# A 96-byte buffer that nothing uses, in front of the shared part of SBUF

## The reference, cut to what matters

```python
h = rms_norm(x, mix_norm[l])
kv = mem_n @ w_mem_kv[l]
mixed, mq = attn_mixer(...) if kind == 0 else lru_mixer(...)
mo = memory_attention(mq, mk, mv)
x = x + jnp.concatenate([mixed, mo], axis=-1) @ w_out[l]
x = x + squared_relu_mlp(rms_norm(x, mlp_norm[l]), w_up[l], w_down[l])   # square(relu(h @ w_up)) @ w_down
```

## Time and profile before

| | |
|---|---|
| time before, median of 3 runs | 3184.8 us (3184.78 to 3188.98) |
| the profiled execution's own time | 3187.99 us |
| its span from first to last instruction | 3186.2 us |
| mean granted TensorE clock | 0.991 |
| PE busy | 3074.7 us (97%) |
| DVE, ACT, POOL busy | 53%, 35%, 3% |
| DMA, share of 16 engines | 17.9% |

### The profile page before, as it was taken

The page is one execution under the profiler, slowest core; times in us unless marked ns, Lnnn a source line. Parts: engine busy times, 40 slices in busy tenths (PEclk is TensorE's granted clock), DMA queues, the critical chain, the costliest instruction groups (busy, mean ns, idle before and its releaser), DMA issues.

```text
span 3186.2 us, 34235 instructions
## 1 busy us (share of the span) xinstructions
PE 3074.7 (97%) x14272; PEld 2383.3 (75%) x14272; DVE 1696.9 (53%) x2180; ACT 1105.2 (35%) x1723; POOL 89.9 (3%) x70
## 2 busy tenths in 40 slices
PE   8998999999999999999999999999999999999898
PEld 7884567788888888777777888888887786666566
DVE  7737854544444433589853633333333733666575
ACT  4215632311111111387732311111111525776552
POOL 0004410000000000000000000000000000000000
PEclk9999999999999999999999999999999999999999
DMA  4420011121222211211131111111111131000213
GB/s 150 114 93 1 1 73 34 53 80 66 67 78 73 73 47 40 93 47 47 53 126 33 47 47 47 47 47 50 49 47 47 53 125 32 22 20 20 93 34 125
DMA packets 54507, 190.94 MB, mean 60 GB/s; under 512 B 6288, under 2 KB 6672, under 8 KB 54224
## 3 DMA queue, kind: packets, MB, share of 16 engines
q1 hardware_dynamic: 54352, 188.74, 17.9%
HBM read 172.73 MB, written 14.68 MB: 59 GB/s over the span
## 4 chain that ended last, share of the span: by engine, by line
PE 75%; DVE 12%; ACT 10%; issue 2%; DMA 0%; POOL 0%; SPq 0%; DVEq 0%; ACTq 0%; POOLq 0%
PE PS L262 62%; PE PS L317 3%; DVE sm L854 1%; PE PS L833 1%; DVE p L1459 1%; ACT p L872 1%; PE PS L819 1%; PE PS L2120 1%; PE PS L2137 1%; DVE wsp L224 1%; PE PS L845 1%; ACT wsp L216 1%; PE PS L1028 1%; PE PS L1036 1%; PE PS L2111 1%
## 5 line engine op out<-in xcount | busy, mean ns | idle before, releaser
L262 PE MATMUL PS<-H,wsp 128*128 128x512 f32 x6864 | 1609.6, 394 | 31.6 <-DVE H L421 9.3
L262 PEld LDWEIGHTS PS<-H,wsp 128*128 128x128 f32 x6864 | 1287.3, 189 | 339.0 <-issue 41.3
L262 PE MATMUL PS<-p,wsp 128*128 128x512 f32 (+1 forms) x3840 | 896.7, 393 | 21.6 <-DVE p L1270 15.1
L262 PEld LDWEIGHTS PS<-p,wsp 128*128 128x128 f32 x3840 | 710.8, 189 | 199.1 <-ACT wsp L216 21.5
L216 ACT ACTIVATE wsp<-raw 128x1024 fp32r<-128x1024 f32 (+1 forms) x267 | 277.0, 1041 | 705.4 <-PE PS L262 640.2
L224 DVE TENSOR_TENSOR wsp<-raw,wsp 128x1024 fp32r<-128x1024 f32 (+1 forms) x267 | 321.7, 1207 | 161.1 <-ACT wsp L216 160.7
L1298 DVE TENSOR_TENSOR p<-p,PS 128x1024 f32<-128x1024 f32 x120 | 146.5, 1221 | 393.7 <-PE PS L262 393.7
L1240 ACT ACTIVATE p<-p 128x1024 fp32r<-128x1024 f32 x64 | 67.9, 1062 | 596.7 <-DVE p L1267 596.7
L1264 DVE TENSOR_TENSOR p<-PS,p 128x1024 f32<-128x1024 f32 x64 | 78.4, 1225 | 317.3 <-PE PS L262 317.2
L872 ACT ACTIVATE p<-PS,sm 128x256 f32<-128x256 f32 (+2 forms) x256 | 128.0, 509 | 173.3 <-DVE sm L860 92.8
L1270 DVE TENSOR_TENSOR p<-p 128x1024 fp32r<-128x1024 f32 x64 | 78.5, 1226 | 72.2 <-ACT p L1240 72.2
(11 more groups left out here) (210 smaller groups left out, 2204.7 us busy)
## 6 DMA issues: line engine op xcount, KB each, us to landing
raw<-in_in_dram SPq DMA_DIRECT2D x72, 512.0 KB, 3.5
raw<-in_dn_dram SPq DMA_DIRECT2D x65, 512.0 KB, 3.5
raw<-in_up_dram SPq DMA_DIRECT2D x64, 512.0 KB, 3.5
raw<-in_out_dram SPq DMA_DIRECT2D x42, 512.0 KB, 3.5
p<-in_ada_dram SPq DMA_DIRECT2D x24, 512.0 KB, 4.4
p<-in_x_dram SPq DMA_DIRECT2D x16, 512.0 KB, 7.6
raw<-in_kv_dram SPq DMA_DIRECT2D x16, 512.0 KB, 3.5
spill_dram<-p SPq DMA_DIRECT2D x16, 512.0 KB, 3.0
```

The source lines that it names most:

```text
L262: ins = e.matmul(ps[:, c:c + m], weights(b, j, wi), x[:, c:c + m], start=first and i == 0, stop=end and i == 2)
```

## The change

One line allocates a tile of 24 float32 (96 bytes) per partition after `sm`. No instruction reads or writes it. What is allocated after it, which is the whole shared part, starts 96 bytes further on, at byte 124544, which is 128 bytes past a multiple of 512. No instruction is added, removed or reordered.

```diff
@@ -165,6 +165,7 @@
         sm = sb("sm", [128, 160])
         ident, ones, invf = cf[:, 128:256], cf[:, 256:384], cf[:, 384:385]
         identb, maskL, maskR, maskD, zerob = (cb[:, i * 128:(i + 1) * 128] for i in range(5))
+        sb("line", [128, 24])
         PS = ctx.enter_context(nc.psum_tensor("PS", [128, 8, 512], F32))
         names = [0]
 
```

## The result

The changed kernel takes 3161.53 us, the median of four runs (3159.09 to 3165.07), against 3185.83 us before in the same comparison (3184.78 to 3188.98): a ratio of 0.9921, 95% interval 0.9905 to 0.9937. That is 24.3 us less (20 to 30 by the interval); 3161 and a sum of 23.5 us were forecast. One execution of the kernel before, 5073.69 us at a granted clock of 0.555, is left out of all medians here. The profiled execution took 3159.09 us with a span of 3157.3, where the one before took 3187.99 with 3186.2, so these two lie 28.9 us apart.

The account below looks back on a forecast made before the run. The prediction took PE, busy 97% of the span, to bound the kernel. Its terms, 19.6 + 2.9 + 0.8 + 0.6 - 0.4 = 23.5 us, brought the median from 3184.8 to 3161 us, range 3153 to 3174.

Parts of the forecast that it names:

- MLP down, 15 groups: Down projections of both layers' MLPs: 174 matmuls per group each save 7.5 ns, 1.31 us per group, 19.6 us.
- memory part of both out projections: Out projections, 192 matmuls each with a shared-part tile moving: 7.5 ns saved per matmul, 2.9 us together.
- halves: The 16th down group, done in halves: 111 matmuls on the chain in one piece save 7.5 ns each, 0.8 us.
- memory values: Line 317 with the memory tile stationary: 96 matmuls fall from 233.3 to 226.7 ns, 0.6 us gained.
- memory keys: Products of 256 columns with the shared part moving: 192 matmuls rise 2.1 ns each, 0.4 us lost.
- LRU, `triR`, scores, transposes, DVE, POOL, DMA: LRU and stick-breaking products, plain float32 products, other engines and loads: each counted 0, with small possible gains or losses.
- The anchoring of the wait: MLP groups: PE's wait for DVE's line 1270 grows from 0.81 to about 0.95 us, absorbing what 18 early matmuls save.
- The float32 products: Scores, values and transposes in plain float32 with shared-part tiles: no surcharge to remove, 0; loss end 2 to 2.5 us.
- the 0.9 us of the upper end: First `x` tile's load at the start: at most 0.9 us gained once, counted 0 in the sum.
- Rival 2: F32R streams with the shared part: period longer than 512 bytes, only half fall into step; 3173 us, chance 0.04.
- Rival 1: Shared part: something other than phase, such as its place above byte 124448, sets the 7.5 ns; 3184.8 us, chance 0.09.
- Rival 3: PE's F32R streams with the shared part: in-step reads collide more often, 2.1 ns each, 9.2 us lost; 3194 us, chance 0.03.

Follow-up runs that it names:

- the streams alone: Two kernels without the model, timing runs of 24, then 64, equal matmuls at chosen operand addresses, against no kernel; they took 238.78 and 394.02 us.

## Why the prediction was right, step by step

The first deciding step, that the price goes with the tile's place and not with the depth of the contraction or the line, came from two rows of line 317, in different stages, that use a different stationary tile at the same depth. The second, that "place" means the phase, was argued from the rows before and not shown by them, which is why the prediction kept "no change" as its first rival. Both held: 226.7 ns after, in the out projection and on line 318, and as much taken off each MLP group as that rate gives.

| term | forecast | measured |
|---|---|---|
| MLP down, 15 groups | 19.6 us | 10.4 + 9.3 = 19.7 |
| memory part of both out projections | 2.9 | 1.46 + 1.42 |
| halves | 0.8 | 1.7 to 1.9, the clock included |
| memory values | 0.6 | 0.6 |
| memory keys | -0.4 | -0.2 (192 x 1.0 ns) |
| LRU, `triR`, scores, transposes, DVE, POOL, DMA | 0 | none told from the clock |

The anchoring of the wait was right: the wait of 0.81 us became 0.94 (0.95 forecast), so only the 174 and not all 192 matmuls of a group paid out. The halves measured more than forecast because the piece of 111 matmuls lay in a stretch of lower clock before; the kernel with 32 bytes of pad gained 1.3 us there without being in step, so how much of the 0.8 came isn't shown. The keys' loss was worked out from a row of line 317 with another stationary tile (120.9), and the streams alone give 120.0 in step. The float32 products were priced at nothing, and the streams alone confirm that the phase doesn't matter to them (429.2 ns a record at 0 and at 32). But the argument misread its rows: line 1036's four records in 1.72 us are two matmuls, 860 ns each or 1.68 ns a column, nearly four times the 0.443 of F32R and not less than twice it. The loads gained nothing: 5.15 us for the first tile where it was 5.05, so the 0.9 us of the upper end was not there. The forecast's median is the measured one within a microsecond; with an interval of 20 to 30 us for the gain, that closeness is luck, and the terms are what was right.

What the prediction had wrong is its wording of the cause. It spoke of a phase against 512 which the shared part was to share with `wsp` and `H`; that is sufficient, but the runs 128 and 256 bytes apart show the period to be 256. The rows before could not have told: weight pieces 512 bytes apart meet `H` at multiples of 512 only. Rival 2 asked for a period above 512 and was wrong. Rival 1 (the shared part's place) fell with the rows of the out projection, and so did the rule of the Trainium skill, "SBUF — State Buffer" (section "Door 1: The DMA port swizzle", note on cachelines): starts that are all multiples of 16 differ by up to 7.6 ns in the streams alone (226.7 to 234.3), so its line size isn't what sets this price. Rival 3 carried over the one row that went the other way, 256 columns; 512 columns with 128 weight columns were never slower in step.

## What to carry to other kernels

Where the same F32R shape has two rates in one profile, compare rows that differ in one operand's buffer alone, and divide distances of starts and not durations. Then look at the address difference of the two operands: here it had to be a multiple of 256 bytes for 512 columns by 128 weight columns, whatever the starts (multiples of 32) were, and one small unused buffer was enough. Before adding the saved nanoseconds up, take out the matmuls that run ahead of an anchored wait, since they only lengthen it.

## What was not expected of the hardware

An F32R matmul of 512 columns by 128 weight columns settles at 226.7 ns, one of 384 at 173.3, one of 256 at 120.0 in step: with N columns that is N/2.4 (one column a cycle at 2.4 GHz) plus 13.3 ns each time, so the fixed part doesn't grow with the columns. A bfloat16 one of 512 takes 215.8. By the Trainium skill, "TensorE: Matmul & The Clock Gate" (section "Back-to-back issue gap"), an isolated matmul's gap is N/2.4 + 2.5, which is 215.8 ns at 512 columns; it puts a stream's lower, at about 131 ns. The bfloat16 stream here takes the isolated figure and not the lower one, and F32R lies 10.9 ns above it in step and 13 to 21 out of it. At 256 columns being 32 or 64 bytes out of step helps (116.7 and 117.8 ns for 120.0). With under 128 weight columns a stream in step no longer reaches 226.7: with 96 it still gains 3.3 ns over being 32 bytes apart, with 16 it loses 0.7.
